# Scores of the differential heads on 64 rows: from one insertion per head to one per pair of heads

## What is computed

```python
qd = q_diff.reshape(B, S, DIFF_HEADS, 2, DIFF_QK)      # DIFF_QK = 64
kd = k_diff.reshape(B, S, DIFF_HEADS, 2, DIFF_QK)
vd = v_diff.reshape(B, S, DIFF_HEADS, DIFF_V)          # DIFF_V = 128
s = jnp.einsum('bqhcd,bkhcd->bchqk', qb, k).astype(jnp.float32) * scale
s = s - slopes[None, None, :, None, None] * dist[:, None, None]
s = jnp.where(causal[None, None, None], s, NEG_INF)
p = jax.nn.softmax(s, axis=-1)
a = p[:, 0] - lam * p[:, 1]
out = jnp.einsum('bhqk,bkhd->bqhd', a.astype(v.dtype), v)
o_diff = (rms_norm(o_diff, g_subln[l]) * (1.0 - lambda_init)).reshape(B, S, DIFF_WIDTH)
y_diff = (o_diff * jax.nn.silu(gate_diff)) @ w_o_diff[l]
```

## Time and profile before

| what | value |
|---|---|
| median of 3 runs | 765.11 us (764.71 to 765.16) |
| the profiled execution's own time | 764.76 us |
| its span (first to last instruction) | 763.0 us |
| PE busy | 752.8 us, 99% |
| weight loads of PE (PEld) busy | 625.1 us, 82% |
| DVE busy | 560.3 us, 73% |
| ACT busy | 424.3 us, 56% |

### The profile page before, as it was taken

How to read it: one execution, slowest core, us unless ns; L and a number is a source line. 1 busy time by engine, 2 the same in 40 slices (tenths; PEclk the granted TensorE clock), 3 DMA queues, 4 the chain that set the end, 5 groups by cost and what they waited for, 6 DMA issues and landing times.

```text
span 763.0 us, 10086 instructions
## 1 busy us (share of the span) xinstructions
PE 752.8 (99%) x3681; PEld 625.1 (82%) x3681; DVE 560.3 (73%) x823; ACT 424.3 (56%) x618; POOL 22.2 (3%) x95
## 2 busy tenths in 40 slices
PE   7999999999999999999999999999999999999997
PEld 5778888888888988888888888888888888888885
DVE  4899998888779579888987768776554556465554
ACT  5689777767656554544545664655444444444441
POOL 2000000000000000000000000011100000000001
PEclk9999999999999999999999999999999999999999
DMA  9999999999584788888886575555556656567642
GB/s 338 395 393 395 357 378 375 339 375 314 172 246 127 219 277 303 290 284 275 295 287 191 163 216 179 168 167 165 187 172 196 191 184 201 186 207 248 221 160 110
DMA packets 132555, 189.71 MB, mean 249 GB/s; under 512 B 10325, under 2 KB 68122, under 8 KB 132250
## 3 DMA queue, kind: packets, MB, share of 16 engines
q1 hardware_dynamic: 132240, 188.77, 74.0%
q10 hardware_dynamic: 266, 0.30, 0.1%
HBM read 185.90 MB, written 2.10 MB: 246 GB/s over the span
## 4 chain that ended last, share of the span: by engine, by line
PE 96%; SPq 2%; DMA 1%; ACT 1%; DVE 0%; issue 0%; DVEq 0%; ACTq 0%
PE ps L1923 17%; PE ps L1925 17%; PE ps L1924 17%; PE ps L1913 16%; PE ps L1899 8%; PE ps L1882 8%; PE ps L1885 4%; SPq L526 2%; PE ps L1718 1%; DMA w_raw<-in_w_in 1%; PE ps L1703 1%; PE ps L1733 1%; PE ps L1876 1%; PE ps L1875 1%; PE ps L1873 1%; PE ps L1692 0%
## 5 line engine op out<-in xcount | busy, mean ns | idle before, releaser
L1569 DVE TENSOR_TENSOR w_both<-w_raw,w_both 128x1024 fp32r<-128x1024 f32 x248 | 301.9, 1222 | 160.6 <-ACT w_both L1036 159.1
L1036 ACT CAST w_both<-w_raw 128x1024 fp32r<-128x1024 f32 x248 | 258.9, 1050 | 239.4 <-PE ps L1925 183.0
L1913 PE MATMUL ps<-w_both,h_both 128*128 128x512 f32 x560 | 138.5, 389 | 0.0
L1913 PEld LDWEIGHTS ps<-w_both,h_both 128*128 128x128 f32 x560 | 105.1, 188 | 22.2
L1923 PE MATMUL ps<-w_both,h_both 128*128 128x512 f32 x296 | 116.8, 395 | 0.0
L1925 PE MATMUL ps<-w_both,h_both 128*128 128x512 f32 x296 | 115.4, 390 | 0.0
L1924 PE MATMUL ps<-w_both,h_both 128*128 128x512 f32 x296 | 115.2, 389 | 0.0
L1899 PE MATMUL ps<-w_both,h_both 128*128 128x512 f32 x280 | 76.0, 393 | 1.0 <-ACT h_both L992 0.7
L1314 DVE SCALAR_TENSOR_TENSOR ada_acc<-ada_ring,cols,ada_acc 128x512 f32<-128x512 f32 x98 | 69.6, 745 | 0.5
L1923 PEld LDWEIGHTS ps<-w_both,h_both 128*128 128x128 f32 x296 | 55.6, 188 | 12.7 <-issue 1.7
L1925 PEld LDWEIGHTS ps<-w_both,h_both 128*128 128x128 f32 x296 | 55.6, 188 | 11.7
(11 more groups left out here) (266 smaller groups left out, 849.3 us busy)
## 6 DMA issues: line engine op xcount, KB each, us to landing
w_raw<-in_w_in SPq DMA_DIRECT2D x177, 512.0 KB, 4.5
ada_ring<-in_w_ada SPq DMA_DIRECT2D x128, 256.0 KB, 6.8
gate_ring<-in_w_ada SPq DMA_DIRECT2D x32, 512.0 KB, 5.1
w_raw<-in_w_out SPq DMA_DIRECT2D x32, 512.0 KB, 3.8
w_raw<-in_w_o_mla SPq DMA_DIRECT2D x16, 512.0 KB, 3.7
w_raw<-in_w_o_diff SPq DMA_DIRECT2D x16, 512.0 KB, 4.1
w_raw<-in_w_ukv SPq DMA_DIRECT2D x16, 256.0 KB, 3.4
x_tok<-in_x SPq DMA_DIRECT2D x2, 1024.0 KB, 6.4
```

What stands on the lines that cost most here:

```text
L1036: act.copy(w_hi[:, p % RING, :], w_raw[:, p % RING, :]).then_inc(hi_done, 1)
L1569: dve.tensor_tensor(w_lo[:, p % RING, :], w_raw[:, p % RING, :], w_hi[:, p % RING, :].bitcast(F32), ALU.subtract).then_inc(lo_done, 1)
L1913: ins = mm(ps[:, b0 + t, :], lhsT=side[:, 2 * i + r, t * P:(t + 1) * P], rhs=w[:, p % RING, r * CH:(r + 1) * CH], start=False, stop=last a ...
```

## The change

The differential scores are made for two heads, 2u and 2u + 1, in one insertion: 8 matmuls on 64 rows at four places, in place of 4 at eight. The 128-key parts of the two heads share banks 6 and 7, the 256-key parts banks 4 and 5. The turned weights go into the score banks (bank 4 for even heads, 5 for odd), and into a second buffer `probsT_odd` for odd heads. Values of differential heads move to the upper half of bank 7, turned outputs to that of bank 6. `DIFF0` is one piece later (126); both heads of a pair have their scores' place at `DIFF0 + 10u` and their weights turned at `DIFF0 + 10u + 5`; values and outputs keep their places of five pieces a head. The offsets of ACT's and DVE's parts (s + 4, s + 6, s + 7, t + 4) are unchanged, so both heads' parts stand at the same piece. `first_scale` has four slots, the bias instruction on DVE is split by key part, and the scores wait for what was read from banks 6 and 7.

```diff
@@ -227,7 +227,7 @@
         cols = sb("cols", [P, NVEC + 3], F32)
         causal = sb("causal", [P, P], F32)
         ratio = sb("ratio", [P, 2, TOK], F32)
-        first_scale = sb("first_scale", [P, 2, 2, TOK], F32)
+        first_scale = sb("first_scale", [P, 4, 2, TOK], F32)
         room(17 * KB - at[0])
         w_raw = sb("w_raw", [P, RING, PIECE], F32)
         w_both = sb("w_both", [P, RING, 2, PIECE], F32R)
...
@@ -260,7 +260,8 @@
         knT = sb("knT", [P, HEADS, SEQ], F32, r_a + 12 * KB)
         v_mla = sb("v_mla", [P, TOK, HEADS, NOPE], F32, r_a + 20 * KB)
         krT = sb("krT", [P, SEQ], F32, r_a + 30 * KB)
-        ones_r = sb("ones_r", [P, P], F32R, r_a + 31 * KB)
+        probsT_odd = sb("probsT_odd", [P, KEYS], F32, r_a + 30 * KB)
+        ones_r = sb("ones_r", [P, P], F32R, r_a + 30 * KB + KEYS * 4)
         merged = sb("merged", [P, TOK, D], F32, r_a)
         post_gain = sb("post_gain", [P, D], F32, r_a + 16 * KB)
         ckv_part = sb("ckv_part", [P, TOK, CH], F32, r_a + 24 * KB)
...
@@ -436,17 +437,29 @@
 
 
         MLA0 = first_piece("uk", 0) + 7
-        DIFF0 = first_piece("mm", 0) + 4
+        DIFF0 = first_piece("mm", 0) + 5
         mla_at = [(MLA0 + h // 2 * 8, MLA0 + 4 * h + 4, MLA0 + 4 * h + 8, MLA0 + 4 * h + (12 if h < HEADS - 1 else 10))
                   for h in range(HEADS)]
-        diff_at = [(DIFF0 + 5 * h, DIFF0 + 5 * h + 5, DIFF0 + 5 * h + 10, DIFF0 + 5 * h + (15 if h < HEADS - 1 else 13))
-                   for h in range(HEADS)]
+        diff_at = [(DIFF0 + h // 2 * 10, DIFF0 + h // 2 * 10 + 5, DIFF0 + 5 * h + 10,
+                    DIFF0 + 5 * h + (15 if h < HEADS - 1 else 13)) for h in range(HEADS)]
         heads_at = mla_at + diff_at
         out_at = sorted({at[2] for at in heads_at} | {at[3] for at in heads_at})
 
         def values_made(m):
 
             return out_at.index(heads_at[m][2]) + 1
+
+        def values_in(m):
+
+            return ps[:, 7, 0:SEQ] if m < HEADS else ps[:, 7, SEQ:2 * SEQ]
+
+        def output_in(m):
+
+            return ps[:, 7 if m < HEADS else 6, SEQ:2 * SEQ]
+
+        def turned_probs(m):
+
+            return probsT if m < HEADS or m % 2 == 0 else probsT_odd
 
         def turned_out(m):
 
...
@@ -840,16 +853,18 @@
         def act_copy_probs(m):
             def run(eng):
                 eng.wait_ge(pT_made, m + 1)
-                if m >= 1:
-                    eng.wait_ge(out_made, values_made(m - 1))
-                act.copy(probsT[:, :], ps[:, 6, 0:KEYS]).then_inc(pT_copied, 1)
+                used = m - 1 if m <= HEADS else m - 2
+                if m >= 1 and m != HEADS + 1:
+                    eng.wait_ge(out_made, values_made(used))
+                bank = 6 if m < HEADS else 4 + m % 2
+                act.copy(turned_probs(m)[:, :], ps[:, bank, 0:KEYS]).then_inc(pT_copied, 1)
             return run
 
         def act_o_hi(m):
             def run(eng):
                 eng.wait_ge(out_made, turned_out(m))
                 scale = 1.0 if m < HEADS else cols[:, NVEC:NVEC + 1]
-                act.activation(o_hi[:, m, :], ps[:, 7, SEQ:2 * SEQ], ACT.Copy, scale=scale).then_inc(o_hi_ready, 1)
+                act.activation(o_hi[:, m, :], output_in(m), ACT.Copy, scale=scale).then_inc(o_hi_ready, 1)
             return run
 
         def act_gate_hi(n):
...
@@ -1214,11 +1229,16 @@
             def run(eng):
                 if m % 2 == h % 2 and m >= 2:
                     eng.wait_ge(pT_made, m - 1)
-                eng.wait_ge(scores_ready, m + 1)
+                eng.wait_ge(scores_ready, HEADS + 2 * (h // 2 + 1))
+                if diff_at[h][0] in out_at:
+                    eng.wait_ge(out_made, out_at.index(diff_at[h][0]) + 1)
                 dst = probs[:, m % 2, :, :]
-                link(eng, dve.scalar_tensor_tensor(
-                    out=dst, in0=dist[:, :].unsqueeze(1).to_broadcast([P, 2, KEYS]),
-                    scalar=-SLOPES[h] / DIFF_SCALE, in1=ps[:, 4:6, 0:KEYS], op0=ALU.mult, op1=ALU.add))
+                for bank, lo, keys in ((6, 0, P), (4, P, SEQ)):
+                    ins = dve.scalar_tensor_tensor(
+                        out=dst[:, :, lo:lo + keys], in0=dist[:, lo:lo + keys].unsqueeze(1).to_broadcast([P, 2, keys]),
+                        scalar=-SLOPES[h] / DIFF_SCALE, in1=ps[:, bank:bank + 2, h % 2 * keys:(h % 2 + 1) * keys],
+                        op0=ALU.mult, op1=ALU.add)
+                link(eng, ins)
                 dve.tensor_reduce(maxes[:, m % 2, 0:2], dst[:, :, 0:P], AX_X, ALU.max).then_inc(scores_read, 1)
                 link(eng, dve.tensor_reduce(maxes[:, m % 2, 2:4], dst[:, :, P:KEYS], AX_X, ALU.max))
                 by_map = lambda x: x[:, m % 2, :].rearrange("p (b w) -> p b w", w=2)
...
@@ -1708,29 +1730,40 @@
                              start=False, stop=t == TOK - 1, skip_group_check=True)
                 ins.then_inc(scores_ready, 2)
 
-            def diff_scores_pe(h):
-                if h == 0:
+            def diff_scores_pe(u):
+
+                place = diff_at[2 * u][0]
+                if u == 0:
                     pe.wait_ge(acc_read_dve, dve_reads("kd", 3))
                 else:
-                    pe.wait_ge(scores_read, h)
+                    pe.wait_ge(scores_read, 2 * u)
+                pe.wait_ge(pT_copied, sum(at[1] < place for at in heads_at))
+                pe.wait_ge(o_gated_ready, sum(at[2] < place for at in heads_at))
+                pe.wait_ge(o_lo_ready, sum(at[3] < place for at in heads_at))
+                pe.wait_ge(gate_copied, sum(at < place for at in gate_sum_at))
                 for w in range(2):
-                    for t, (lo, keys) in enumerate(((0, P), (P, SEQ))):
-                        ins = mm(ps[:, 4 + w, lo:lo + keys], lhsT=qdT[w * DQK:(w + 1) * DQK, h, t * P:(t + 1) * P],
-                                 rhs=kdT[w * DQK:(w + 1) * DQK, h, 0:keys], start=True, stop=True)
-                ins.then_inc(scores_ready, 1)
+                    half = slice(w * DQK, (w + 1) * DQK)
+                    for h in (2 * u, 2 * u + 1):
+                        for t, bank, keys in ((0, 6, P), (1, 4, SEQ)):
+                            ins = mm(ps[:, bank + w, h % 2 * keys:(h % 2 + 1) * keys], lhsT=qdT[half, h, t * P:(t + 1) * P],
+                                     rhs=kdT[half, h, 0:keys], start=True, stop=True)
+                ins.then_inc(scores_ready, 2)
 
             def transpose_probs(m):
                 if m < HEADS:
+                    bank = 6
                     pe.wait_ge(exps_done, m + 1)
+                    if m >= 1:
+                        pe.wait_ge(pT_copied, m)
+                    sums = sum(place < heads_at[m][1] for place in gate_sum_at)
+                    if sums:
+                        pe.wait_ge(gate_copied, sums)
                 else:
+                    bank = 4 + m % 2
                     pe.wait_ge(weights_ready, m - HEADS + 1)
-                if m >= 1:
-                    pe.wait_ge(pT_copied, m)
-                sums = sum(place < heads_at[m][1] for place in gate_sum_at)
-                if sums:
-                    pe.wait_ge(gate_copied, sums)
+                    pe.wait_ge(scores_read, (m - HEADS) // 2 * 2 + 2)
                 for k in range(3):
-                    ins = tr(ps[:, 6, k * P:(k + 1) * P], probs[:, m % 2, 0, k * P:(k + 1) * P], ident[:, :])
+                    ins = tr(ps[:, bank, k * P:(k + 1) * P], probs[:, m % 2, 0, k * P:(k + 1) * P], ident[:, :])
                 ins.then_inc(pT_made, 1)
 
             def values(m):
...
@@ -1793,6 +1830,8 @@
             pe_after[PH1 + 3].append(turn_kr)
             for g in range(N_GROUPS):
                 pe_after[group_at[g][0]].append(lambda g=g: group(g))
+            for u in range(HEADS // 2):
+                pe_after[diff_at[2 * u][0]].append(lambda u=u: diff_scores_pe(u))
             for m, place in enumerate(heads_at):
                 pe_after[place[3]].append(lambda m=m: transpose_out(m))
             for m, place in enumerate(heads_at):
...
@@ -1802,7 +1841,6 @@
             for h in range(HEADS):
                 if h % 2 == 0:
                     pe_after[mla_at[h][0]].append(lambda h=h: mla_scores(h // 2))
-                pe_after[diff_at[h][0]].append(lambda h=h: diff_scores_pe(h))
             for n in range(4):
                 pe_after[merge_at[n]].append(lambda n=n: transpose_merged(n))
                 pe_after[gate_sum_at[n]].append(lambda n=n: gate_sum(n))
```

More of the change, by code:

```diff
@@ L665, in head_root @@
                 pool.wait_ge(head_root_ready, h + 1)
-                nc.gpsimd.tensor_tensor(rstd[:, k, :], rstd[:, k, :], first_scale[:, h % 2, 1, :], ALU.mult).then_inc(rstd_ready, 1)
+                nc.gpsimd.tensor_tensor(rstd[:, k, :], rstd[:, k, :], first_scale[:, h % 4, 1, :], ALU.mult).then_inc(rstd_ready, 1)
                 pool.wait_ge(rstd_ready, k)
@@ L1201, in run @@
             def run(eng):
-                src = ps[:, 7, SEQ:2 * SEQ]
+                src = output_in(m)
```

(26 more changed lines are left out.)

## The result

The changed kernel takes 772.41 us (median of 5 runs, 772.02 to 772.55), the kernel before 764.84 us in the same comparison (5 runs). The ratio is 1.0093, with a 95% interval from 1.0081 to 1.0104: 0.9% slower, 7.6 us. The forecast was 769.7 us, slower by 4.6.

What follows compares the result with a forecast made beforehand. PE, busy 99% of the span, was taken to bound the kernel. Insertions -1.6 us and late weights +6.2 us gave +4.6 on the 765.11 us median, so 769.7 us, with a range of 766.0 to 772.6.

Steps and rivals of the forecast that it cites:

- What bounds the kernel: PE is busy throughout 386 to 534 us, so time changes only through PE's work or PE's waits.
- Term 2: Before PE turns a pair's weights, PE waits 1.09 us in pair 0, 1.50 in the others; with hand-overs, 6.2 us lost.
- Term 1: Score insertions on PE: eight at 1.06 us become four of twice the content at 1.72, gaining 1.6 us.
- A pair then costs 1.72: Cost in us of one two-head score insertion on PE: doubled content of 0.66, plus entry and exit 0.40.
- the halves no longer run side by side: Rival at the score matmuls: the halves run one after the other, 3.04 us a pair, 775.0 us; chance 0.06.
- The outer bound of the term, 1.92: Pair's score insertion in us if the second head's content costs the whole 0.86; the gain is then 0.8.
- Costed at nothing: DVE's split bias, later casts, new waits ahead of the scores and extra buffers were taken to add no time.
- No wait: Rival: both heads' weights are ready when PE comes to turn them, so only the insertions count; 763.5 us, chance 0.07.
- half the wait: Rival: PE's waits before turning the weights come to 3 us or less, 766.5 us at most; chance 0.11.
- The case that got the chance of 0.76: The forecast itself: cheaper score insertions and late weights both as worked out, with own bounds of 768.2 and 772.6 us.

Runs made afterwards that it cites:

- run 2: Against the changed kernel, PE turns both heads' weights six pieces behind the scores in place of five; 766.30 us.
- run 3: Against the changed kernel, DVE makes a pair's weights one piece earlier, ahead of the low part that follows the exps; 766.20 us.
- run 7: Against the changed kernel, ACT makes the odd head's exps one piece later, behind the next cast; 766.05 us.
- run 5: Against the changed kernel, weights turned six pieces behind the scores, and score matmuls changing half at every matmul; 763.25 us.
- run 6: As run 2, but with three matmuls of the first half ahead of the second half's first three, then the fourth of each; 764.95 us.
- run 1: Against the changed kernel, only the score matmuls reordered: per head, two on rows 0-63, then two on rows 64-127; 769.81 us.

## Why the prediction was right, and where a step failed

**What bounds the kernel: right.** With PE at 148.00 of 148.00 us, what PE waited and worked more was found again in the span (6.5 + 1.2 against 7.7 us).

**Term 2, the late weights: right in mechanism, place and nearly in size.** Forecast 1.09 us in the first pair and 1.50 in the others, with 0.15 for each stop 1.24 and 1.65; the trace shows 1.11, 1.65, 1.63 and 1.64. Forecast in all 6.2 us, measured 6.5 by the wait rows and 6.1, 6.2 and 6.4 by the runs that removed them (2, 3 and 7). The parts of the sum held: the table load ahead of the pair's exps (1.28 us), eight exps in a row (478.69 to 482.2, where ACT's timeline has the next cast start, 3.5 us), the second head's weights 1.26 us behind the first's (485.03 and 486.29), DVE's weights as the releaser. Runs 3 and 7 show that the chain through the cast and the low part was the reason; the forecast had counted those as given and hadn't said that they were needless.

**Term 1, the insertions: wrong, in size and sign.** The step that failed is "A pair then costs 1.72", and in it the claim that the halves run side by side whatever their order. It cost 2.42: -1.6 us turned into +1.2. Entry, exit and content were sized well: with the halves together (run 5) a pair costs 1.51 + 0.15 = 1.66, and the four save 8.5 - 6.7 = 1.8 us by the chain, 1.6 by the clock. What was missed is that the order puts all of one half ahead of the other. I had this as the rival "the halves no longer run side by side", at 3.04 a pair and a chance of 0.06, and dismissed it because four passes ahead did no harm. That was no evidence on eight. Its evidence for the overlap was also read too strongly: 32 records of 377 ns come to 12.1 us, but two passes of one half that follow each other overlap in the trace as well (starts 0.218 us apart), so with the halves fully apart the group would be busy for 16 x 0.595 = 9.5 us, an estimate from these two numbers. The 4.9 us still showed halves side by side; the 7.6 us of the changed kernel lie between. So did the cost: one half works alone for 0.765 us at either end, not all the time. The outer bound of the term, 1.92, was too narrow by the same mistake.

**Costed at nothing: right.** Run 2 shows no new wait when the weights are no longer in the way: DVE's split bias, the later casts, the waits ahead of the scores and the new banks cost nothing that can be seen.

**Rivals.** "No wait" and "half the wait" fall with the wait rows. The rule of the Trainium skill named there ("TensorE: Matmul & The Clock Gate", section "The mechanism"), program order in start and end of matmuls, would have the second half of the changed kernel begin after the start of the first half's eighth pass; it begins at the fifth, and in the kernel before at the first.

The time fell inside the range, 0.2 us from its upper end, and that was partly luck. The two terms' errors, +2.8 and +0.3 us, point the same way. The upper end of 772.6 had been made of 0.8 us for a dearer pair, 0.6 for dearer hand-overs and 1.5 for late casts; run 2 shows no late casts, and the error of term 1 alone was 2.8. The case that got the chance of 0.76, both terms as worked out, came true in its second term only.

## What to carry to other kernels

In these runs float32 matmuls on different halves of the array's rows overlapped fully only where they stood near each other in the program. So change the row half at every matmul (1.51 us here), or at least every second one (1.61), above all when insertions are merged: four of one half ahead of the other cost 2.27. When work is merged, look not only at its sum but at what now stands ahead of its result on each engine: here the second head's exps pushed a cast, the cast a low part, and the result stood behind both, though it needed neither. Shifting the consumer by one piece, or the producer past one unneeded step, was worth 6 us; merging, with the halves in a good order, 1.6.

## What the runs showed of the hardware that was not expected

The runs show how far PE reaches past waiting matmuls of the busy half of its rows to start one of the free half. A float32 score matmul shows as two records ("passes") in the trace. The table gives the passes of the first half ahead of the second half's first, and when that one started, for the first head or pair:

```
passes ahead   second half starts   beside the first half's   scores in the chain
4 (before)     0.013 us             first pass                0.86 us (one head)
6 (run 6)      0.330 us             third pass                1.84 us (two heads)
8 (changed)    0.765 us             fifth pass                2.27 us (two heads)
2 (run 5)      0.007 us             first pass                1.51 us (two heads)
```

In the three cases with four or more, the second half starts when just three passes of the first have not started yet. For the kernel before this is a lower bound, since its second half could hardly have started earlier. Whether the limit counts matmuls, weight loads or both wasn't told apart. With two matmuls of a half given out at a time (run 1) the second head's halves drift 0.11 us apart; changing at each keeps them 0.006 to 0.007 us apart.
